# A two-layer hybrid decoder step on one core: the four group passes of layer 0 written as a loop whose passes overlap

## The chip, the cores and the metric

The kernel runs on one core of one Trainium2 chip. The metric is the device time of that core in microseconds (us), from the start of the program to its end, so lower is better. The engines are named as the profile names them: PE is TensorE (matmuls, and PEld its weight loads), DVE is VectorE, ACT is ScalarE, POOL is GpSimd, and SP is SyncE, which here only issues DMAs. Each engine works through its own list of instructions strictly in order. Semaphores are the only link between the engines: `wait_ge(s, n)` holds an engine, with everything behind it, until `s` has reached `n`.

## The reference

520 tokens (512 of a prompt and 8 decoding samples) with 1024 features pass through layer 0, a Mamba-2 mixer, and layer 1, a gated short convolution, and a last RMSNorm. Only layer 0 is touched by the change:

```python
def ssd_mixer(h, conv_buf, ssm_state, w_in, conv_w, conv_b, dt_bias, A_log, Dskip, norm_w, w_out):
    proj = h @ w_in
    z, xBC, dt = proj[..., :D_INNER], proj[..., D_INNER:D_INNER + SSD_CONV_DIM], proj[..., D_INNER + SSD_CONV_DIM:]
    xBC, new_buf = causal_dwconv(xBC, conv_buf, conv_w)      # 4 taps, per channel
    xBC = jax.nn.silu(xBC + conv_b)                          # -> xs, Bm, Cm
    dt = jax.nn.softplus((dt + dt_bias).astype(jnp.float32))
    A = -jnp.exp(A_log.astype(jnp.float32))
    y, new_state = ssd_chunked(xs, dt, A, Bm, Cm, ssm_state) # per chunk of 128 tokens
    y = y + Dskip[:, None] * xs
    y = y.reshape(b, L, D_INNER) * jax.nn.silu(z)
    y = grouped_rmsnorm(y, norm_w, SSD_GROUPS)               # one norm for each of 4 groups
    return y @ w_out, new_buf, new_state
```

All data is float32. `ssd_chunked` has, for each of 32 heads, a product within chunks of 128 tokens, the states of the chunks, a recurrence over the four chunks, and a product of the earlier state with C.

## The kernel before

**Numbers in halves.** Features lie on the partitions and tokens along the free axis, 520 columns as two halves of 260. Each float32 operand of a large matmul is split into a rounded "high" part (`whi`, `hhi`, `yhi`) and the rest (`wlo`, `hlo`, `ylo`), and a product is three matmuls: high by high, high by low, low by high. The high part of a weight chunk is a copy on ACT (L475, `split_next` and `split_out`), the low part a subtraction on DVE (L826, `next_low`).

**Chunks.** The weights come as chunks of 512 KB, numbered in the order of the table `LAYER0`. A chunk is 48 matmuls of 260 columns (L1348 for the projections B, C, x0 to x3, z0 to z3 of a group; L1380 for `o0` to `o3`, the output projection of the group before). SP loads chunk n into `raw[n % 2]` when chunk n-2 has been split into both parts, and the split parts lie in four slots, so chunk n+4 is split when PE has finished chunk n. The results go to two pairs of PSUM banks in turn (`PAIR`), and a pair must be evacuated before PE may write it again: projections by ACT (L556 to L560, `evac_conv`, or `evac_z`), outputs by DVE, which adds them to the residual (L942 and L943, `residual0`; an `o` chunk takes two turns, one for each half of its 256 columns).

**Passes.** Layer 0 is a loop over the four groups, written out in the program. In a pass, each of B, C, x0 to x3 goes through evacuation, the first tap and a tanh on ACT, and three taps (L958, `conv`) and a `silu` (L967) on DVE. Then for each q from 0 to 3 (two heads): `turn(q)` on PE transposes x, `weigh_dt` on DVE and `weigh` on POOL make `xd` and `xdd`; `within(q)` on PE has the chunk states (L1438) and the product within chunks (L1447, with `em`, which ACT makes and DVE masks in `causal`, L981); `recur` on DVE (L985 and L989) runs the recurrence; `across(q)` on PE (L1457) adds the earlier state, which DVE weighs and adds in `add_earlier`; `gate` on DVE (L1040) multiplies with silu(z) (L1033). The samples' state is scaled on ACT (L622), gets its new term by POOL (L402, `inject`) and DVE (L1022, `sample_add`), and is read by POOL (L407, `read_out`) and DVE (L1026, `sample_out`). The squares of the gated y are summed on POOL (`add_squares`, L424), PE adds them over the partitions (L1391, `group_sums`), ACT makes the root (L460 to L466, `logs` and `roots`), DVE scales (L923, `norm_scale`) and splits y (L930, `y_low`); the `o` chunks of the next pass need it.

**The order.** Nothing but the order of the calls sets what stands where on an engine. In the kernel before, all four gates of a group come before the first conv of the next group on DVE, and the squares' sums come on PE after chunks B and C of the next group. The steps that turn dt into decays (`dt_v` and `dt_s` count them) stand on DVE, ACT and PE (`columns`) before anything of the first pass that follows chunk C.

## Time and profile before

| | us |
|---|---|
| median of 3 runs | 1053.88 (1052.34 to 1056.37) |
| the profiled execution | 1050.48 |
| its span, first to last instruction | 1048.8 |
| PE busy | 920.6 (88%) |
| DVE busy | 667.7 (64%) |
| ACT busy | 477.4 (46%) |
| POOL busy | 164.0 (16%) |
| mean granted clock of PE | 0.942 of full |

Busy times are sums of the recorded instructions of an engine. Matmuls overlap in the records, so a single one lasts longer there than it holds the engine; what a chunk costs is read from the start of its first matmul to the start of what follows. The granted clock is given as a share of full speed: 1.0 is 2.4 GHz, and the other level, 1.2 GHz, is 0.5, so 0.90 in a stretch says that PE ran a fifth of it at the lower level.

### The profile page before, as it was taken

The page shows a single profiled execution, that of the slowest core. Times are in us where ns is not written, and L with a number is a line of the kernel's source. Part 1 is how long each engine was busy: PE and PEld are TensorE (multiplying, and loading weights), DVE is VectorE, ACT ScalarE, POOL GpSimd, SP SyncE. Part 2 cuts the span into 40 slices and gives each one's busy share as a digit, 9 for nine tenths or more (in the row PEclk, how much of TensorE's full clock was granted, in tenths as well). Part 3 has the DMA queues.
Part 4 walks back from the last instruction along what each step waited for, and adds up shares of the span by engine and source line. Part 5 has one row for each costly group of instructions (what it writes and reads, how often), then busy time and mean ns, then how long its engine had stood idle before and what let it go on. Part 6 is the DMA issues. An engine that isn't in the chain of part 4 may idle for free.

```text
span 1048.8 us, 19245 instructions
## 1 busy us (share of the span) xinstructions
PE 920.6 (88%) x7371; PEld 900.7 (86%) x7371; DVE 667.7 (64%) x1072; ACT 477.4 (46%) x885; POOL 164.0 (16%) x101
## 2 busy tenths in 40 slices
PE   5899688688787888868689999999999999989996
PEld 5698687688786878868679999999999999989996
DVE  5679987856868579687945454554445455463543
ACT  5477656534465354665434443232333233243444
POOL 6303540213402234022700000000000000000000
PEclk7899889899898898989879999999999999999999
DMA  7135444343443434434312243223323322331212
GB/s 187 44 113 171 127 135 114 119 123 84 123 121 124 123 83 124 119 125 144 106 43 79 62 122 98 80 84 108 88 83 97 100 80 80 103 97 62 101 58 82
DMA packets 162923, 107.98 MB, mean 103 GB/s; under 512 B 5024, under 2 KB 155068, under 8 KB 162300
## 3 DMA queue, kind: packets, MB, share of 16 engines
q1 hardware_dynamic: 123876, 76.15, 24.9%
q10 hardware_dynamic: 38592, 30.54, 10.0%
q0 software_dynamic: 400, 0.55, 0.3%
q8 instruction: 35, 0.57, 0.2%
q14 instruction: 20, 0.16, 0.0%
HBM read 95.35 MB, written 12.14 MB: 102 GB/s over the span
## 4 chain that ended last, share of the span: by engine, by line
PE 57%; DVE 24%; ACT 6%; issue 6%; POOL 2%; DVEq 0%; POOLq 0%; ACTq 0%
PE bank L1348 43%; PE bank L1528 9%; DVE acc L958 5%; DVE wlo L826 4%; PE bank L1380 4%; DVE zh L1033 2%; DVE turned L989 2%; DVE sample L1022 1%; DVE yr L1026 1%; DVE xd L972 1%; ACT whi L475 1%; ACT thx L570 1%; ACT em L594 1%; POOL sample L402 1%; DVE dtx L1016 1%
## 5 line engine op out<-in xcount | busy, mean ns | idle before, releaser
L1348 PE MATMUL bank<-hhi,whi 128*128 128x260 f32 x1664 | 347.4, 291 | 39.0 <-DVE xT L943 34.3
L1348 PE MATMUL bank<-hlo,whi 128*128 128x260 f32 x1664 | 342.0, 288 | 0.0
L1348 PE MATMUL bank<-hhi,wlo 128*128 128x260 f32 x1664 | 341.4, 287 | 0.0
L1348 PEld LDWEIGHTS bank<-hhi,whi 128*128 128x128 f32 x1664 | 265.0, 195 | 44.7 <-DVE xT L943 36.1
L1348 PEld LDWEIGHTS bank<-hlo,whi 128*128 128x128 f32 x1664 | 264.0, 194 | 0.0
L1348 PEld LDWEIGHTS bank<-hhi,wlo 128*128 128x128 f32 x1664 | 263.4, 193 | 0.0
L475 ACT ACTIVATE whi<-raw 128x1024 fp32r<-128x1024 f32 x136 | 143.6, 1056 | 231.3 <-PE bank L1348 151.3
L826 DVE TENSOR_TENSOR wlo<-raw,whi 128x1024 fp32r<-128x1024 f32 x132 | 171.5, 1301 | 43.6 <-ACT whi L475 41.6
L1380 PE MATMUL bank<-yhi,whi 128*128 128x260 f32 x256 | 55.6, 300 | 15.6 <-issue 5.0
L958 DVE SCALAR_TENSOR_TENSOR acc<-ext,colA,acc 128x544 f32<-128x544 f32 x72 | 66.4, 922 | 3.4 <-ACT acc L564 1.7
L1380 PEld LDWEIGHTS bank<-yhi,whi 128*128 128x128 f32 x256 | 42.0, 201 | 17.2 <-issue 9.3
L407 POOL TENSOR_TENSOR sample<-sample 128x1024 f32<-128x1024 f32 x16 | 43.5, 2717 | 83.4 <-DVE sample L1022 83.4
L394 POOL TENSOR_TENSOR xdd<-xd,dte 128x512 f32<-128x512 f32 x16 | 23.4, 1460 | 210.4 <-DVE xd L972 183.4
L1528 PE MATMUL bank<-hhi,whi 128*128 128x260 f32 x256 | 52.3, 286 | 3.6 <-DVE hlo L1184 3.6
L1380 PE MATMUL bank<-ylo,whi 128*128 128x260 f32 x256 | 53.8, 293 | 0.0
L1380 PE MATMUL bank<-yhi,wlo 128*128 128x260 f32 x256 | 53.8, 293 | 0.0
L1528 PE MATMUL bank<-hlo,whi 128*128 128x260 f32 x256 | 52.1, 285 | 0.0
L1528 PE MATMUL bank<-hhi,wlo 128*128 128x260 f32 x256 | 51.9, 285 | 0.0
L475 ACT ACT_TABLE_LOAD x16 | 20.5, 1283 | 66.1 <-PE bank L1348 66.0
L594 ACT ACTIVATE em<-abc,acol 128x128 f32<-128x128 f32 x128 | 39.0, 388 | 13.8 <-PE bank L1447 10.2
L1528 PEld LDWEIGHTS bank<-hhi,whi 128*128 128x128 f32 x256 | 39.9, 191 | 3.8 <-issue 3.8
L402 POOL TENSOR_TENSOR sample<-sample,dtx 128x1024 f32<-128x1024 f32 x16 | 36.6, 2289 | 35.7 <-DVE yr L1026 29.6
(227 smaller groups left out, 1218.3 us busy)
## 6 DMA issues: line engine op xcount, KB each, us to landing
raw<-in_sc_w_in SPq DMA_DIRECT2D x64, 512.0 KB, 4.0
raw<-in_ssd_w_in SPq DMA_DIRECT2D x40, 512.0 KB, 3.9
abc<-a_rows ACTq DMA_DIRECT2D x16, 512.0 KB, 4.2
sample<-in_state_ssm ACTq DMA_DIRECT2D x16, 512.0 KB, 5.5
out_new_ssm_s<-sample ACTq DMA_DIRECT2D x16, 512.0 KB, 3.5
raw<-in_ssd_w_out SPq DMA_DIRECT2D x16, 512.0 KB, 3.4
raw<-in_sc_w_out SPq DMA_DIRECT2D x16, 512.0 KB, 3.5
sample<-bc_rows ACTq DMA_DIRECT2D x4, 1024.0 KB, 4.7
```

The costliest lines, as they stand in the source:

```text
L394: pool.tensor_tensor(xdd[:, :, :].rearrange("p c (h d) -> p c h d", h=2), xd[:, :, :].rearrange("p c (h d) -> p c h d", h=2), scale, ALU.m ...
L402: pool.tensor_tensor(tdec[:, :, :], bcbc[:, :, 0, :], dtx[:, q % 2, :].unsqueeze(2).broadcast_to([P, NB, NS]), ALU.mult).then_inc(t1_done, 1)
L407: pool.tensor_tensor(tdec[:, :, :], st[:, q % 2, :].rearrange("p (b n) -> p b n", n=NS), bcbc[:, :, 1, :], ALU.mult).then_inc(t2_done, 1)
L475: act.activation(whi[:, slot, :], raw[:, slot % RAW, :], ACT.Copy).then_inc(hi_done, 1)
L594: e = act.activation(em[:, h, c * Q:(c + 1) * Q], abc[:, h, c * Q:(c + 1) * Q], ACT.Relu, scale=-1.0, bias=acol[:, c, ds(g * 8 + (2 * q + ...
L826: dve.tensor_tensor(wlo[:, slot, :], raw[:, slot % RAW, :], whi[:, slot, :].bitcast(F32), ALU.subtract).then_inc(lo_done, 1)
L958: t = dve.scalar_tensor_tensor(acc[:, :], row[:, k:k + CONV0], cw0(k, tile), acc[:, :], ALU.mult, ALU.add)
L989: dve.scalar_tensor_tensor(hs[:, c, h * HD:(h + 1) * HD], hs[:, c - 1, h * HD:(h + 1) * HD], cdbc[:, c, ds(g * 8 + (2 * q + h), 1)], bank[ ...
L1033: dve.scalar_tensor_tensor(zh[:, q % 2, :], th[:, :], 1.0, zh[:, q % 2, :], ALU.add, ALU.mult).then_inc(sz_done, 1)
L1348: mm = pe.matmul(b[:, 0:TH], w[:, slot, k * P:(k + 1) * P], h[:, k, cols], start=(k == 0 and i == 0), stop=(k == KT - 1 and i == 2))
L1380: mm = pe.matmul(bank[2 * p + hb][:, 0:TH], w[:, slot, k * 256 + part * P:k * 256 + (part + 1) * P], y[:, k, hb * TH:(hb + 1) * TH], start ...
L1528: mm = pe.matmul(bank[2 * i + hb][:, 0:TH], w[:, c % SLOT, kk * 512 + i * P:kk * 512 + (i + 1) * P], h[:, r, hb * TH:(hb + 1) * TH], start ...
```

## The change

Layer 0's passes are written as one loop on each engine, whose body begins in the middle of pass g and ends in the middle of pass g+1. Every step takes the pass as an argument and does nothing outside of 0 to 3. The steps themselves are the same instructions, with three differences: a chunk's two halves are now separate calls (`out_part`), the split of a chunk on ACT (`split`) and the first tap (`first_tap`) are calls of their own that can stand away from the evacuation, and `within` is divided into `chunk_states` and `within`. Only `MIDDLE` and `LAST` of the chunk order change: the `o` chunks stand between x3 and z3, one after each z (two of the last pass are named l2 and l3). Waits are added where the order no longer implies them. The dt steps become nine small calls; those that PE, ACT and DVE did before x0 now stand between the first chunks' convolutions. Layer 1, the start and the end are as they were.

```diff
-MIDDLE = ["B", "C", "x0", "x1", "x2", "o0", "x3", "o1", "z0", "o2", "z1", "o3", "z2", "z3"]
-LAST = ["B", "C", "x0", "x1", "x2", "o0", "x3", "o1", "z0", "z1", "z2", "z3", "o2", "o3"]
+MIDDLE = ["B", "C", "x0", "x1", "x2", "x3", "o0", "z0", "o1", "z1", "o2", "z2", "o3", "z3"]
+LAST = ["B", "C", "x0", "x1", "x2", "x3", "o0", "z0", "o1", "z1", "z2", "z3", "l2", "l3"]
...
+            for g in range(-1, GROUPS):
+                proj(g, "z2")
+                chunk_states(g, 2)
+                out_part(g, "o3", 0)
+                turn(g, 3)
+                within(g, 2)
+                out_part(g, "o3", 1)
+                proj(g, "z3")
+                across(g, 2)
+                chunk_states(g, 3)
+                proj(g + 1, "B")
+                out_part(g, "l2", 0)
+                across(g, 3)
+                within(g, 3)
+                proj(g + 1, "C")
+                proj(g + 1, "x0")
+                if g == -1:
+                    spread_decays()
+                out_part(g, "l2", 1)
+                if g == -1:
+                    columns()
+                if g == 3:
+                    turn_tails()
+                group_sums(g)
+                proj(g + 1, "x1")
+                turn_B(g + 1)
+                out_part(g, "l3", 0)
+                turn_bc(g + 1)
+                proj(g + 1, "x2")
+                turn(g + 1, 0)
+                cb_products(g + 1)
+                proj(g + 1, "x3")
+                out_part(g, "l3", 1)
+                chunk_states(g + 1, 0)
+                out_part(g + 1, "o0", 0)
+                turn(g + 1, 1)
+                within(g + 1, 0)
+                out_part(g + 1, "o0", 1)
+                across(g + 1, 0)
+                proj(g + 1, "z0")
...
+            def evac_conv(g, e):
...
+                act.wait_ge(proj_done, NUMBER[g, CONVED[e]] + 1)
+                if g * 6 + e > 1:
+                    act.wait_ge(conv_done, g * 6 + e - 1)
...
+            def split(g, what):
+                if (g, what) not in NUMBER:
+                    return
+                n = NUMBER[g, what]
+                act.wait_ge(proj_done, n + 1)
                 high(n + SLOT, n % SLOT, ((n + SLOT) // RAW + 1) * 16)
...
+                gate(g - 1, 3)
+                conv(g, 0)
+                silu(g, 0)
+                if g == -1:
+                    dt_bias()
+                next_low(g - 1, "z3")
+                next_low(g, "B")
+                conv(g, 1)
+                norm_scale(g - 1, 0)
+                if g == 0:
+                    decays_to_end()
+                silu(g, 1)
+                if g == 0:
+                    by_channel()
```

Three places of the new order follow. The first is DVE where pass 1 ends and pass 2 begins. In the rows, `sample` and `yr` are the samples' state and its sum, `ybuf<-ybuf,zh` the gate, `acc` the taps, `turned` the silu of B or C, `ybuf<-ybuf,colB,sqs` the norm's scaling. Before:

```order
L1026 TENSOR_REDUCE yr<-sample 128x1024
L1029 TENSOR_TENSOR ybuf<-ybuf,yr 128x8
L1040 TENSOR_TENSOR ybuf<-ybuf,zh 128x520
L958 SCALAR_TENSOR_TENSOR acc<-ext,colA,acc 128x544 x3
L967 SCALAR_TENSOR_TENSOR turned<-thx,acc 128x544
L826 TENSOR_TENSOR wlo<-raw,whi 128x1024
L958 SCALAR_TENSOR_TENSOR acc<-ext,colA,acc 128x544 x3
L967 SCALAR_TENSOR_TENSOR turned<-thx,acc 128x544
```

And after the change, at the same place:

```order
L1302 TENSOR_REDUCE yr<-sample 128x1024
L1306 TENSOR_TENSOR ybuf<-ybuf,yr 128x8
L1322 TENSOR_TENSOR ybuf<-ybuf,zh 128x520
L1131 SCALAR_TENSOR_TENSOR acc<-ext,colA,acc 128x544 x3
L1152 SCALAR_TENSOR_TENSOR turned<-thx,acc 128x544
L1014 TENSOR_TENSOR wlo<-raw,whi 128x1024 x2
L1131 SCALAR_TENSOR_TENSOR acc<-ext,colA,acc 128x544 x3
L1160 SCALAR_TENSOR_TENSOR ybuf<-ybuf,colB,sqs 128x520
L1152 SCALAR_TENSOR_TENSOR turned<-thx,acc 128x544
L1160 SCALAR_TENSOR_TENSOR ybuf<-ybuf,colB,sqs 128x520 x2
```

The conv of B still stands right behind the last gate. What moved is the scaling, now mixed with the silu of C, and two low parts that stand behind B's silu.

The second place is ACT at the same seam: `ext` and `tail` are the evacuation, `acc` the first tap, `whi` a high part, `thx` the tanh. Before:

```order
L560 ACTIVATE ext<-cst 128x8x3
L564 ACTIVATE acc<-ext,colA 128x544
L475 ACTIVATE whi<-raw 128x1024
L570 ACTIVATE thx<-acc 128x544
L556 ACTIVATE ext<-bank 128x260
```

And after the change:

```order
L595 ACTIVATE ext<-cst 128x8x3
L604 ACTIVATE acc<-ext,colA 128x544
L591 ACTIVATE ext<-bank 128x260
L592 ACTIVATE ext<-bank 128x252
L593 ACTIVATE ext<-bank 128x8
L594 ACTIVATE tail<-bank 128x11
L595 ACTIVATE ext<-cst 128x8x3
L506 ACTIVATE whi<-raw 128x1024 x2
L747 DMA out_new_ssm_s<-sample 128x8x128
L657 DMA abc<-a_rows 128x1024
L611 ACTIVATE thx<-acc 128x544
```

B's tanh now stands behind C's evacuation and two high parts.

The third place is DVE at the first `o` chunk of pass 2: `xT` is the residual that frees a pair of banks, `turned<-turned,cdbc,bank` the recurrence, `em` the mask, `xs` the silu of an x chunk. Before:

```order
L958 SCALAR_TENSOR_TENSOR acc<-ext,colA,acc 128x544 x3
L942 TENSOR_TENSOR xT<-xT,bank 128x260
L943 TENSOR_TENSOR xT<-xT,bank 128x260
L981 TENSOR_TENSOR em<-em,turned 128x1024
L967 SCALAR_TENSOR_TENSOR xs<-thx,acc 128x544
L942 TENSOR_TENSOR xT<-xT,bank 128x260
L943 TENSOR_TENSOR xT<-xT,bank 128x260
```

And after the change:

```order
L1131 SCALAR_TENSOR_TENSOR acc<-ext,colA,acc 128x544 x3
L1235 COPY turned<-bank 128x128
L1239 SCALAR_TENSOR_TENSOR turned<-turned,cdbc,bank 128x64 x6
L1184 TENSOR_TENSOR xT<-xT,bank 128x260
L1185 TENSOR_TENSOR xT<-xT,bank 128x260
L1014 TENSOR_TENSOR wlo<-raw,whi 128x1024
L1295 TENSOR_TENSOR sample<-sample 128x1024
L1215 TENSOR_TENSOR xd<-bank,dtcol 128x512
```

The two residuals that stood together, an `em` mask and a silu apart, are now spread, and the first stands behind the recurrence of q = 0; on PE, `turn(1)`, `within(0)`, the other half of the chunk and `across(0)` stand between the first half and z0, the next user of its banks.

## Rows read from the trace of the kernel before

**Rows 1.** Busy time by stretch: length, PE, PEld, DVE, ACT, POOL, clock, DMA, GB/s.

```profile
36.00:146.00 110.00, 91.75 (x744) 87.38 (x742) 95.46 (x143) 67.32 (x163) 38.32 (x19) 0.92 0.45 133
146.00:278.00 132.00, 106.36 (x830) 103.20 (x830) 97.25 (x144) 67.45 (x158) 33.51 (x18) 0.91 0.40 114
278.00:410.00 132.00, 107.00 (x830) 103.58 (x830) 98.13 (x146) 67.44 (x158) 34.80 (x18) 0.90 0.41 114
410.00:526.00 116.00, 88.32 (x690) 85.15 (x691) 92.55 (x137) 65.66 (x153) 35.63 (x18) 0.90 0.39 117
575.00:936.00 361.00, 360.06 (x2994) 359.60 (x2993) 184.62 (x351) 120.94 (x116) 0.00 (x0) 1.00 0.31 90
```

**Rows 2.** Groups by line, PE, 146 to 526 us: busy, mean ns | idle before.

```profile
L1348 PE MATMUL bank<-hhi,whi 128*128 128x260 f32 x448 | 100.7, 309 | 34.3 <-DVE xT L943 34.3
L1380 PE MATMUL bank<-yhi,whi 128*128 128x260 f32 x176 | 37.7, 297 | 11.9 <-issue 5.0 <-ACT ext L560 4.3 <-ACT zh L579 2.6
L1438 PE MATMUL bank<-xdd,turned 128*128 128x128 f32 x96 | 13.6, 287 | 6.1 <-POOL xdd L394 6.1
L1391 PE MATMUL bank<-sqs,ones 128*128 128x260 f32 x13 | 7.1, 690 | 21.4 <-POOL sqs L424 21.4
```

**Rows 3.** The chain that ended last: start, us, what.

```profile
320.64 8.78 PE bank L1348 x48
...
369.58 5.98 PE bank L1380 x48
375.56 5.74 PE bank L1348 x48
```

**Rows 4.** Timeline of PE, one step of q in pass 2.

```profile
329.26 0.27 PE L1286 MATMUL bank<-ident,turned 128*128 128x128 f32 x1
...
332.46 0.49 PE L1380 MATMUL bank<-yhi,whi 128*128 128x260 f32 x2
```

**Rows 5.** Groups by line and shape, DVE, 272 to 404 us.

```profile
L826 DVE TENSOR_TENSOR wlo<-raw,whi 128x1024 fp32r<-128x1024 f32 x15 | 22.6, 1510 | 0.3 <-ACT whi L475 0.3
...
L1033 DVE SCALAR_TENSOR_TENSOR zh<-th,zh 128x520 f32<-128x520 f32 x5 | 9.6, 1912 | 0.0
...
L1022 DVE TENSOR_TENSOR sample<-sample 128x1024 f32<-128x1024 f32 x4 | 4.9, 1219 | 1.8 <-POOL sample L402 1.8
...
L923 DVE SCALAR_TENSOR_TENSOR ybuf<-ybuf,colB,sqs 128x520 f32<-128x520 f32 x4 | 2.8, 754 | 2.3 <-ACT sqs L466 2.3
```

**Rows 6.** Timelines of POOL and DVE in pass 2: three meetings, one without.

```profile
337.65 2.36 POOL L407 TENSOR_TENSOR sample<-sample 128x1024 f32<-128x1024 f32 x1 [15.99 <-DVE sample L1022]
...
338.09 1.95 DVE L1016 TENSOR_TENSOR dtx<-xs,dtch 128x8 f32<-128x8 f32 x1
...
354.56 3.30 POOL L407 TENSOR_TENSOR sample<-sample 128x1024 f32<-128x1024 f32 x1 [5.03 <-DVE sample L1022]
...
355.53 2.88 DVE L1033 SCALAR_TENSOR_TENSOR zh<-th,zh 128x520 f32<-128x520 f32 x1
...
372.24 0.69 DVE L1033 SCALAR_TENSOR_TENSOR zh<-th,zh 128x520 f32<-128x520 f32 x1
...
389.72 2.42 POOL L407 TENSOR_TENSOR sample<-sample 128x1024 f32<-128x1024 f32 x1 [1.34 <-DVE sample L1022]
389.88 1.49 DVE L989 SCALAR_TENSOR_TENSOR turned<-turned,cdbc,bank 128x64 f32<-128x64 f32 x6
```

**Rows 7.** High parts on ACT, and the weights' DMA, from the page.

```profile
L475 ACT ACTIVATE whi<-raw 128x1024 fp32r<-128x1024 f32 x136 | 143.6, 1056 | 231.3 <-PE bank L1348 151.3
...
raw<-in_ssd_w_in SPq DMA_DIRECT2D x40, 512.0 KB, 3.9
```

**Rows 8.** Timeline of DVE at the start of pass 0.

```profile
48.71 0.81 DVE L899 TENSOR_TENSOR em<-ident,sm 32x640 f32<-32x640 f32 x1
...
54.58 2.43 DVE L958 SCALAR_TENSOR_TENSOR acc<-ext,colA,acc 128x544 f32<-128x544 f32 x3 [1.70 <-ACT acc L564]
```

**Rows 9.** The chain again, from the last group's sums into layer 1.

```profile
525.70 2.10 PE bank L1391 x4
...
539.03 7.29 PE bank L1380 x48
...
570.24 12.49 PE bank L1348 x102
```

More of the change, by code:

```diff
@@ new lines, in _ @@
+            next_low(3, "o0")
+            sample_add(3, 1)
+            sample_x(3, 2)
+            silu_z(3, 0)
+            residual0(3, "o1", 1)
+            skip(3, 1)
+            weigh_dt(3, 2)
+            gate(3, 0)
+            next_low(3, "z0")
+            silu(3, 5)
+            next_low(3, "o1")
+            weigh_earlier(3, 1)
+            sample_out(3, 1)
+            add_earlier(3, 1)
+            causal(3, 2)
+            next_low(3, "z1")
+            recur(3, 2)
+            sample_add(3, 2)
@@ new lines, in out_part @@
+                pe.wait_ge(pair_free[p], turn + 1)
+                for k in range(STEPS):
+                    pe.wait_ge(yg_hi, (g - 1) * STEPS + k + 1)
+                    pe.wait_ge(yg_lo, (g - 1) * STEPS + k + 1)
+                    for i, (w, y) in enumerate(((whi, yhi), (whi, ylo), (wlo, yhi))):
+                        for hb in range(2):
+                            mm = pe.matmul(bank[2 * p + hb][:, 0:TH],
+                                           w[:, slot, k * 256 + part * P:k * 256 + (part + 1) * P],
+                                           y[:, k, hb * TH:(hb + 1) * TH],
+                                           start=(k == 0 and i == 0), stop=(k == STEPS - 1 and i == 2))
@@ new lines, in cb_products @@
+            def cb_products(g):
+                if g not in PASSES:
+                    return
+                pe.wait_ge(silu_done, g * 6 + 3)
+                if g == 0:
+                    pe.wait_ge(dt_v, 23)
+                else:
+                    pe.wait_ge(rec, g * 28)
+                for c in range(NC):
+                    mm = pe.matmul(bank[5][:, c * Q:(c + 1) * Q], BT[:, c * Q:(c + 1) * Q], CT[:, c * Q:(c + 1) * Q],
+                                   start=True, stop=True)
+                mm.then_inc(cb_done, 1)
@@ new lines, in chunk_states @@
+            def chunk_states(g, q):
+                if g not in PASSES:
+                    return
+                i = g * STEPS + q
+                pe.wait_ge(xdd_done, i + 1)
+                pe.wait_ge(bs_done, g + 1)
+                if q == 0:
+                    pe.wait_ge(cbm_done, g + 1)
+                else:
+                    pe.wait_ge(rec, 7 * i)
+                for c in range(NC):
+                    mm = pe.matmul(bank[5][:, c * P:(c + 1) * P], Bs[:, c, :], xdd[:, c, :], start=True, stop=True)
+                mm.then_inc(s_done, 1)
@@ new lines, in within @@
+            def within(g, q):
+                if g not in PASSES:
+                    return
+                i = g * STEPS + q
+                pe.wait_ge(m_done, i + 1)
+                pe.wait_ge(xd_done, i + 1)
+                if q == 0:
+                    pe.wait_ge(bcd_done, g + 1)
+                else:
+                    pe.wait_ge(yd_done, 2 * i)
+                for c in range(NC):
+                    for h in range(2):
+                        mm = pe.matmul(bank[6][h * HD:(h + 1) * HD, c * Q:(c + 1) * Q], xd[:, c, h * HD:(h + 1) * HD],
+                                       em[:, h, c * Q:(c + 1) * Q], start=True, stop=True)
+                mm.then_inc(sd_done, 1)
@@ new lines, in across @@
+            def across(g, q):
+                if g not in PASSES:
+                    return
+                i = g * STEPS + q
+                pe.wait_ge(rec, 7 * (i + 1))
+                pe.wait_ge(yo_done, i + 1)
+                pe.wait_ge(fin_done, i + 1)
+                if i == 0:
+                    pe.wait_ge(dt_s, 8)
+                elif q == 0:
+                    pe.wait_ge(ln_done, g + 1)
+                transpose(bank[7][:, 0:NS], hs[:, NC - 1, :])
+                for c in range(1, NC):
+                    mm = pe.matmul(bank[7][:, c * Q:(c + 1) * Q], hs[:, c - 1, :], CT[:, c * Q:(c + 1) * Q],
+                                   start=True, stop=True)
+                mm.then_inc(o_done, 1)
```

1475 lines of the change are left out of this document (860 added, 615 removed).

## The prediction

> **What bounds the kernel now.** I read the table of stretches first, cut at the places where PE sums the squares of a group, since each pass comes through that place once [rows 1]. It shows three kinds of stretch. Layer 1 (575 to 936 us) has PE busy for 360.1 of 361 us at clock 1.00: nothing there can be gained by an order, and the change does not touch it. The four passes of layer 0 are different. In pass 1 (146 to 278) and pass 2 (278 to 410), 132 us each, PE is busy for 106.4 and 107.0 us at a granted clock of 0.91 and 0.90, and DVE for 97.3 and 98.1. So neither engine is full, and they stop each other. Only the first pass has DVE near its limit: 95.5 us of 110.
>
> Next the groups of PE over 146 to 526 us, for what it waits for [rows 2]: 34.3 us for DVE's residual, which frees a pair of banks, 21.4 us for POOL's sums of squares, 11.9 us before `o` chunks, 6.1 us for `xdd`. That is 73.7 us over three passes. Then the chain, for what a wait costs afterwards [rows 3]: a chunk takes 5.74 us, but the chunk that begins at 320.64, behind a long wait for the residual, takes 8.78. The chunk at 369.58 takes 5.98, so a short wait leaves the clock where it was. A wait is thus paid for twice when it is long: itself, and up to 3.0 us of a chunk at the lower level, 1.2 GHz.
>
> **What the floor of a pass is.** A middle pass has 14 chunks of 5.74 us, 80.4 us. One step of q (across, chunk states, within, transpose) goes from 329.26 to 332.46, 3.2 us [rows 4], four times 12.8. The sums take 2.1 [rows 9], and B's transposes and the products of B and C about 1 (estimate: half as many small matmuls as a step, less the rest). That is 96.3 us. A second way gives the same: 107.0 us busy at clock 0.90 is 96.3 at full clock [rows 1]. DVE's work is 98 us as it stands, of which some is time in which POOL held it up: the 15 low parts take 1.51 us in the mean, where an operation of the same size and kind (L1022) takes 1.22, and the silus of z take 1.91 where one that met nobody takes 0.69 [rows 5, 6]. These two groups alone are 4.4 + 6.1 = 10.5 us; with other groups of that kind I take 15 us (estimate), so DVE's own work is about 83 us a pass, and POOL's is 35.
>
> **The change, part by part.** No matmul, no DVE operation on data and no DMA is added or removed, apart from the division of calls; a wait that is satisfied costs less than I can read. So all of the gain is in when things stand.
>
> *The residuals.* Before, the two residuals of o0 stand behind a conv and a mask, and PE has only within(0) and turn(1) before it needs the banks. After, half a chunk (2.9 us) and a step's matmuls lie between each half and the next user of its pair, and DVE does a residual between other work. I laid PE's new order out at 5.74 a chunk, 2.87 a half and 3.2 a step, with time 0 at x2, and then DVE's list beside it, each step at its duration in the timeline of pass 2 (a low part 1.14, a conv 2.42, a residual 0.67, a recurrence 1.7, start to start, where they met nobody). The first half of o0 is done at 16.6; DVE gets to its residual by 20.9, behind recur(0); z0 wants the banks at 21.7. The second half is done at 20.9, the residual at 26.1, wanted by o1 at 28.4. o1's: 33.5 against 35.6, and 39.6 against 41.3. So the 34.3 us go, but with slack of 0.8 to 2.3 us, and POOL's collisions will eat this in some places. *The squares.* The gate of q = 3 comes at 81.2 in this frame, POOL ends about 3 us later, and PE sums at 88.3, since chunk x0 has moved ahead of the sums. The 21.4 us go in passes 1 and 2. *xdd and the chunk states*: 12.2 against 12.8, and 26.5 against 27.5: gone, with almost no slack.
>
> *What becomes late next.* At the seam ACT makes B's tanh behind C's evacuation and two high parts of 1.06 us each [rows 7], so DVE, whose silu of B stands right behind B's conv, waits until about 3.7 us after PE ends C; behind it in DVE's list stand the low parts for x1 and x2, and PE waits for them if they slip by 2 us. I read 2.6 us of waiting for DVE there. The norm's scaling stood behind the root before, with 2.3 us of waiting [rows 5], and the same 2.4 us stay. The recurrence of q = 3 waits for its chunk states behind z3, about 3 us in this frame, which later collisions fill. So a pass is 98.1 us of DVE as now (the collisions are those of now: the same operations meet) + 2.4 + 2.6 + 3 for all places where PE and DVE miss each other by little, 106 us. PE has then some 10 us of idle time in pieces too short to lower the clock. Ends of this: PE's floor, 96.3, and DVE's 83 with all of POOL's 35 on top, 118. I take 106 since the walk found no wait of PE over 2.5 us, and since 98.1 is measured and not argued.
>
> *How POOL and DVE collide* decides between these. POOL's `read_out` ran from 337.65 to 340.01, and DVE's product of 8 columns at 338.09 took 1.95 us and ended when POOL did; the silu of z at 355.53 took 2.88 and ended within 0.6 us of POOL. But the recurrence at 389.88, one of whose inputs is in PSUM, ran its usual 1.49 us beside POOL [rows 6]. The Trainium skill, page "SBUF — State Buffer", section "SBUF: two separate sides", states that the two engines take one pair of ports as an exclusive lock, where DVE has two inputs in SBUF. By that rule the trace agrees, and it speaks against this change: the fuller DVE is, the more of POOL's time falls on it.
>
> *The last pass* (410 to 526) has DVE busy for 92.6 of 116 us. The same additions give 92.6 + 8 = 100.6, less 2.4 for a conv that moves across the cut, plus 2 for the end, where nothing of a next pass fills the gaps: 100. *The first pass* is DVE's: it starts its first conv at 54.58 now, since ACT evacuates B only behind the dt steps, while its last dt product starts at 48.71 and ends at 49.5 [rows 8]. After, ACT evacuates B and C early, and conv B can start at about 50. The decays it then does between convs take as long as before. I take 4.6 us; the ends are 0, if the added waits for `dt_s` and `dt_v` hold PE's transposes, and 10, if the pass also loses its few gaps. *The end* of layer 0, 525.7 to 570.24 [rows 9], has a chunk of 7.29 us at the lower clock and a last low part that PE awaits; spreading it gives 3 us, with ends of 0 and 8.
>
> **The sum.** 4.6 + (132 - 106) x 2 + (116 - 100) + 3 = 75.6 us. The profiled execution took 1050.5 us, so 974.9; the median of the runs shown is 3.4 us above it, so **978 us**. With the waits at 106 +/- 4 a pass and the last pass alike, its own range is 965 to 992.
>
> **Rivals.** *A, DVE is the bound and POOL falls on it whole* (chance 0.17). A pass is 83 + 35 = 118, the last 92.6 - 15 + 35.6 = 113: 4.6 + 28 + 3 + 3 = 39 us, 1015. For it: the low parts and the silus of z show how often the two meet already [rows 5]; against: the recurrence went past POOL unharmed [rows 6], and so should the residuals and other readers of PSUM. The lock that the Trainium skill states on the page "SBUF — State Buffer" is this rival's mechanism, and taken alone it gives these 1015 us, where the measured busy time gives 978.
>
> *B, PE's floor is reached* (0.13). 97 us a pass and 92 for the last: 4.6 + 70 + 24 + 8 = 107, 947. For it: the walk shows PE never waiting if DVE has its durations without collisions; against: the slacks of 0.3 to 2.3 us are less than one collision of 2.2.
>
> *C, slower, by the raw slots* (0.04). Two chunks share the slots in turn, so for each slot a round is a landing of 3.9 us, the high part's 1.06 and the low part's 1.22 [rows 5, 7], 6.2, plus the time a loaded chunk waits for its turn in ACT's list and then in DVE's. A round serves two chunks of PE time. While these queue waits stay below 2 x 6.9 - 6.2 = 7.6 us, they are free. If ACT, which now waits for a `proj_done` at each split, and DVE add 12.8 us between them, a round takes 19, a pass 133, and the kernel ends at 1050 to 1065. In my walk the worst round (split of o3 to its low part, 18 us) has one such wait and not seven.
>
> *D, no change* (0.03): the waits go to other places in the same amount, a pass of 131 us, within 0.5%, about what a measurement of this kernel can tell from no change.
>
> **How the numbers follow.** Own case 0.63, A 0.17, B 0.13, C 0.04, D 0.03. The range reaches to A's and B's times: **948 to 1015**. Faster by more than 0.5%: 0.63 + 0.17 + 0.13 = 0.93; slower 0.04; same 0.03.
>
> **What would show it.** In the changed profile, the sums of the squares should lie some 106 us apart (before: 132), with the granted clock in these stretches at 0.97 or more, and DVE at 92% or more of each pass. PE's wait for the residual should fall from 34.3 to under 12 us, and for POOL's sums from 21.4 to a few, nearly all in the last pass. DVE's longest regular waits should be the silu of B for its tanh and the scaling for the root. First conv at 50. I would be wrong if the low parts and silus of z, in the mean, take much longer than 1.51 and 1.91 us (A), if PE waits for `wlo` or ACT for `raw` in each pass (C), or if a long wait at the seam keeps the clock at 0.9.

## The result, and the profile after

The changed kernel takes **948.41 us** (median of 4 runs, 945.86 to 951.9), the kernel before 1053.11 us in the same series (4 runs, 1052.09 to 1056.37): a ratio of 0.9003, 95% interval 0.8968 to 0.9039, 104.7 us less. The forecast was 978 with a range of 948 to 1015, so the time lies at the very bottom of the range: direction right, size too small. The profiled execution took 951.9 us, the longest of the four; its span is 950.2, the mean granted clock 0.972 (before 0.942).

The table of stretches, cut in each pass at the sums of the squares (columns as in [rows 1]), and layer 1 in the last row:

```profile
36.00:137.00 101.00, 94.98 (x795) 92.58 (x792) 93.60 (x142) 67.77 (x168) 36.90 (x19) 0.97 0.51 144
137.00:237.30 100.30, 97.23 (x832) 94.93 (x831) 97.14 (x145) 67.06 (x158) 32.69 (x17) 1.00 0.52 148
237.30:337.00 99.70, 97.17 (x832) 94.85 (x831) 96.84 (x144) 67.02 (x158) 32.56 (x17) 1.00 0.52 153
337.00:431.40 94.40, 76.77 (x644) 73.92 (x642) 90.74 (x137) 63.20 (x147) 33.76 (x17) 0.94 0.46 140
...
480.00:840.00 360.00, 356.01 (x2959) 355.28 (x2957) 187.96 (x356) 124.10 (x122) 0.00 (x0) 1.00 0.31 92
```

A middle pass holds the same 832 or so matmuls and 97 us of DVE's busy time as before, in 100 us instead of 132. PE's busy time itself falls by 9 to 10 us, since the clock there is 1.00 and no longer 0.90. In layer 1 PE is still 99% busy at clock 1.00.

What PE waits for, its groups over 36 to 470 us, against [rows 2], and then its waits in pass 2 one by one:

```profile
L1700 PE MATMUL bank<-hhi,whi 128*128 128x260 f32 x654 | 136.0, 289 | 5.4 <-DVE wlo L1014 5.4
L1744 PE MATMUL bank<-yhi,whi 128*128 128x260 f32 x256 | 54.7, 295 | 2.2 <-DVE ylo L1169 1.6 <-issue 0.6
L1835 PE MATMUL bank<-em,xd 128*64 128x128 f32 x256 | 18.9, 293 | 10.3 <-DVE em L1224 10.3
...
L1757 PE MATMUL bank<-sqs,ones 128*128 128x260 f32 x16 | 5.2, 459 | 8.7 <-POOL sqs L444 8.7
```

```profile
240.01 0.47 PE L1700 MATMUL bank<-hhi,whi 128*128 128x260 f32 x2 [1.66 <-DVE wlo L1014]
...
268.24 0.33 PE L1638 MATMUL bank<-ident,turned 128*128 128x128 f32 x1 [0.50 <-DVE turned L1239]
...
278.99 1.09 PE L1835 MATMUL bank<-em,xd 128*64 128x128 f32 x16 [0.21 <-DVE em L1224]
```

The wait for the residual, 34.3 us, is gone altogether; the wait for POOL's sums, 21.4, is 8.7 and lies in the last pass alone. In pass 2 PE loses 2.4 us to waits, none of which lowers the clock.

Last, DVE's groups over the two middle passes (137 to 337 us), against [rows 5]:

```profile
L1014 DVE TENSOR_TENSOR wlo<-raw,whi 128x1024 fp32r<-128x1024 f32 x28 | 36.5, 1309 | 0.0
...
L1224 DVE TENSOR_TENSOR em<-em,turned 128x1024 f32<-128x1024 f32 x8 | 16.5, 2067 | 0.0
L1312 DVE SCALAR_TENSOR_TENSOR zh<-th,zh 128x520 f32<-128x520 f32 x8 | 13.3, 1664 | 0.0
...
L1257 DVE TENSOR_SCALAR ybuf<-xs,dch 128x8 f32<-128x8 f32 x8 | 6.2, 769 | 0.0
...
L1160 DVE SCALAR_TENSOR_TENSOR ybuf<-ybuf,colB,sqs 128x520 f32<-128x520 f32 x8 | 5.9, 755 | 1.1 <-ACT sqs L497 1.1
...
L1152 DVE SCALAR_TENSOR_TENSOR turned<-thx,acc 128x544 f32<-128x544 f32 x4 | 2.9, 723 | 1.4 <-ACT thx L611 1.4
L1235 DVE COPY turned<-bank 128x128 f32<-128x128 f32 x8 | 2.3, 282 | 1.0 <-PE bank L1820 1.0
```

DVE's waits on other engines in two passes are the three shown, 3.5 us together.

DVE begins its first conv 4.9 us earlier than in [rows 8], at the row

```profile
49.70 2.41 DVE L1131 SCALAR_TENSOR_TENSOR acc<-ext,colA,acc 128x544 f32<-128x544 f32 x3
```

and the chain from the last sums into layer 1 (start, us, what) answers to [rows 9]; its first chunk still runs at the lower clock, 7.37 us:

```profile
431.38 2.10 PE bank L1757 x4
433.47 7.37 PE bank L1744 x48
...
484.73 5.30 PE bank L1700 x42
```

The gain by stretch, from the marks, which are the starts of the sums (before 146.9, 279.5, 411.0, 525.7; after 137.0, 237.3, 337.0, 431.4), and the start of layer 1's steady chunks (584.5 and 484.7): first pass 9.9 us, middle passes 32.3 and 31.7, last pass 20.4, end of layer 0 5.5. Their sum is 99.8 us. The spans differ by 98.6, since what follows takes 1.2 us longer in the changed kernel.

### The profile page after: what moved, and what is told of

The parts are those of the page before. It is cut to its first block, busy times and chain, and to the rows that moved or that the text cites. A ratio compares the mean times of both kernels' runs of the same rounds, so it can differ in the third digit from the quotient of the medians.

```text
span 950.2 us, 19548 instructions
## 1 busy us (share of the span) xinstructions
PE 893.1 (94%) x7371; PEld 877.8 (92%) x7371; DVE 663.9 (70%) x1072; ACT 475.5 (50%) x885; POOL 157.4 (17%) x101
## 4 chain that ended last, share of the span: by engine, by line
PE 52%; DVE 1%; ACT 1%; issue 0%; POOLq 0%; POOL 0%; DVEq 0%; ACTq 0%
PE bank L1700 39%; PE bank L1935 10%; PE bank L1744 3%; DVE zh L1312 0%; ACT xT L934 0%; POOLq L86 0%; PE bank L1757 0%; DVE ybuf L1628 0%; ACT sqb L774 0%; DVE hlo L1536 0%; ACT L491 0%; DVE yr L1302 0%; ACT whi L506 0%; POOL sqb L432 0%; PE bank L1964 0%
## 5 line engine op out<-in xcount | busy, mean ns | idle before, releaser
L1700 PE MATMUL bank<-hhi,whi 128*128 128x260 f32 x1664 | 339.2, 285 | 6.4 <-DVE wlo L1014 5.4
L1700 PE MATMUL bank<-hhi,wlo 128*128 128x260 f32 x1664 | 336.3, 284 | 0.0
L1700 PE MATMUL bank<-hlo,whi 128*128 128x260 f32 x1664 | 335.6, 283 | 0.0
L1700 PEld LDWEIGHTS bank<-hhi,whi 128*128 128x128 f32 x1664 | 257.8, 190 | 9.1 <-issue 7.6
L1700 PEld LDWEIGHTS bank<-hhi,wlo 128*128 128x128 f32 x1664 | 257.5, 189 | 0.0
L1700 PEld LDWEIGHTS bank<-hlo,whi 128*128 128x128 f32 x1664 | 257.3, 189 | 0.0
L1014 DVE TENSOR_TENSOR wlo<-raw,whi 128x1024 fp32r<-128x1024 f32 x132 | 166.1, 1260 | 38.3 <-ACT whi L506 36.0
L1131 DVE SCALAR_TENSOR_TENSOR acc<-ext,colA,acc 128x544 f32<-128x544 f32 x72 | 62.6, 870 | 1.8
L1935 PE MATMUL bank<-hhi,whi 128*128 128x260 f32 x256 | 53.0, 289 | 3.6 <-DVE hlo L1536 3.6
L1935 PE MATMUL bank<-hlo,whi 128*128 128x260 f32 x256 | 52.5, 287 | 0.0
L1935 PE MATMUL bank<-hhi,wlo 128*128 128x260 f32 x256 | 52.4, 287 | 0.0
L1935 PEld LDWEIGHTS bank<-hhi,whi 128*128 128x128 f32 x256 | 40.5, 194 | 3.8 <-issue 3.8
L416 POOL TENSOR_TENSOR sample<-sample,dtx 128x1024 f32<-128x1024 f32 x16 | 38.8, 2424 | 27.2 <-issue 17.8
L1935 PEld LDWEIGHTS bank<-hlo,whi 128*128 128x128 f32 x256 | 40.7, 194 | 0.0
L1935 PEld LDWEIGHTS bank<-hhi,wlo 128*128 128x128 f32 x256 | 40.4, 193 | 0.0
```

The lines of the kernel that those rows point to most:

```text
L416: pool.tensor_tensor(tdec, bcbc[:, :, 0, :], dtx[:, q % 2, :].unsqueeze(2).broadcast_to([P, NB, NS]), ALU.mult).then_inc(t1_done, 1)
L1014: dve.tensor_tensor(wlo[:, slot, :], raw[:, slot % RAW, :], whi[:, slot, :].bitcast(F32), ALU.subtract).then_inc(lo_done, 1)
L1131: t = dve.scalar_tensor_tensor(acc[:, :], row[:, k:k + CONV0], cw0(k, tile), acc[:, :], ALU.mult, ALU.add)
L1700: mm = pe.matmul(b[:, 0:TH], w[:, slot, k * P:(k + 1) * P], h[:, k, cols], start=(k == 0 and i == 0), stop=(k == KT - 1 and i == 2))
L1935: mm = pe.matmul(bank[2 * i + hb][:, 0:TH], w[:, c % SLOT, kk * 512 + i * P:kk * 512 + (i + 1) * P], h[:, r, hb * TH:(hb + 1) * TH], start ...
```

## Experiments

The open questions: what holds a pass at 100 us now, PE's list of work, or DVE's with POOL's interference; which moves brought the gain; and why the waits that the forecast put on DVE did not come. Each expectation spells out its own theories. Times are medians; ratios are to the kernel before in the same series (1051.81 us for the first four, 1050.34 for the next four, 1051.02 for the last four). The changed kernel itself came out at ratios of 0.9003 and 0.9035 in two series, 3 us apart, so a difference of medians across series is uncertain by about as much; the marks of its two profiled executions agree within 0.2 us.

**1. The dt steps in one block again** (dt_first). All of the changed kernel, but the dt chain stands ahead of the loop on each engine, and the sample columns and decays between chunk C and x0:

```diff
+            dt_exp()
+            dt_log()
+            early_high()
+            ...
             for g in range(-1, GROUPS):
```

> The changed kernel, but all dt steps stand in one block before the loop on ACT and DVE, and PE does columns and decays between C and x0 of pass 0, as in the kernel before. Theory 1 (the head's gain is that the first conv starts at 49.7 instead of 54.6 us, and what follows is dense on DVE either way): first sums of squares at 142, against 137.0 in the changed kernel and 146.9 before; the later intervals stay 100, 100, 94 us; the whole 5 us above the changed kernel, 953. Theory 2 (all 9.9 us of the head come from the dt steps): first sums at 147, the whole 958. Theory 3 (the dt steps were hidden anyway): first sums at 137 to 138, the whole 949.

Measured 953.8 us (953.31 to 954.87), ratio 0.9064 [0.9044, 0.9085]. DVE's first conv starts at 53.53 instead of 49.70, PE waits for ACT's evacuation once more, and the first mark is 141.8, 4.8 us later than 137.0:

```profile
52.67 0.80 PE L1685 MATMUL bank<-hhi,whi 128*128 128x260 f32 x2 [1.85 <-ACT ext L595]
```

So the spreading is worth 5 us up to the first mark. At the last mark (433.5 against 431.4) 2.1 us of it are left: the later passes take 100.5, 98.3 and 92.9 us, the last two 1.4 and 1.5 us less than in the changed kernel, with DVE busy for 1.3 and 0.8 us less. The medians differ by 5.4. The other 5.1 of the 9.9 us that the first pass gained lie elsewhere in it; at its end alone PE waited 3.70 us for POOL's sums before, and does not now.

**2. The sums of the squares where they were** (sums_early), ahead of chunk x0 in the first three passes:

```diff
+                if g < 3:
+                    group_sums(g)
                 proj(g + 1, "x0")
...
-                group_sums(g)
+                if g == 3:
+                    group_sums(g)
                 proj(g + 1, "x1")
```

> The changed kernel, but PE sums the squares of passes 0 to 2 before chunk x0 and not behind it, where the kernel before had it (behind B and C). Theory 1 (the sums waited because PE reached them before DVE's last gate; a chunk of 5.7 us in between covers this): PE waits 3 to 5 us for POOL at each of the three places, and each interval becomes 3 to 5 us longer, 103 to 105, since PE has only 3 us to spare in a pass: the whole 957 to 963. Theory 2 (DVE sets the pace and PE has slack to catch up): the wait of PE shows, but the intervals stay at 100 to 101, the whole 948 to 951.

Measured 957.18 us (955.01 to 958.43), 0.909 [0.9066, 0.9115], the lower end of what was expected. PE waits at each of the three places (4.21, 3.61 and 5.00 us), and the group shows the old wait:

```profile
L1757 PE MATMUL bank<-sqs,ones 128*128 128x260 f32 x16 | 6.5, 547 | 20.4 <-POOL sqs L444 20.4
```

11.7 us more of waiting here cost 7.8 us at the last mark and 8.8 in the medians, since other waits shrink (for `wlo` from 5.4 to 0, for `em` from 10.3 to 8.2): DVE caught up while PE stood. The first three marks stand a chunk earlier in this order, 101.7 and 101.6 us apart, nearer to theory 2's 100 to 101 than to theory 1's 103 to 105.

**3. One residual half about 5 us later** (res_pair): the first half of o0 is added when the second is.

```diff
                 recur(g, 0)
-                residual0(g, "o0", 0)
...
+                residual0(g, "o0", 0)
                 residual0(g, "o0", 1)
```

> The changed kernel, but DVE does the residual of the first half of o0 together with that of the second half, about 5 us later, behind an operation on the samples, xd, the earlier state and the skip, so that z0's banks come free late. Theory 1 (the place of the residual is a large part of the gain): PE waits about 4 to 5 us before z0 in passes 1 to 3 and the intervals become 104, 104, 97: the whole 10 to 14 us above the changed kernel, 958 to 962. Theory 2 (DVE's list alone sets the pace, and PE's wait is made up before DVE needs PE again): waits of 4 us show on PE, but the intervals grow by less than 1.5 us each, the whole 949 to 952.

Measured 962.76 us (960.55 to 964.42), 0.9152 [0.9128, 0.9176]. PE waits 4.4 us in each of three passes. The two middle passes take 105.2 and 104.5 us; the last takes 94.6, against 94.4 in the changed kernel:

```profile
276.35 0.80 PE L1700 MATMUL bank<-hhi,whi 128*128 128x260 f32 x2 [4.39 <-DVE xT L1185]
```

The two matmuls behind it take 0.80 us together, where two behind a short wait take 0.47 (at 240.01 above): the lower clock again (granted 0.50 from 276.3 to 280). The last mark comes 9.2 us later than in the changed kernel for 13.2 us of waiting, since PE's waits for `em` fall from 10.3 to 5.5; the medians differ by 14.3. One of eight residual halves a pass is enough for it. The slack of this half is small, as the walk had it (0.8 us): in pass 2 of the changed kernel the residual ends at 268.86 and z0 begins at 269.00.

**4. The kernel before, with four residuals earlier on DVE** (before_res): in each pass o0's and o1's stand one or two calls further ahead; nothing else is touched.

```diff
+                        residual0(g, 0, 0)
                     conv(4, g * 4 + 2)
-                        residual0(g, 0, 0)
```

> The kernel before, with one thing of the change alone: four calls of the residual on DVE (o0 and o1, both halves, passes 1 to 3) stand earlier: the first half of o0 ahead of the conv of x2 and the second ahead of the mask, those of o1 around the silu of x3. Theory 1 (places of the residuals are a third of the gain): PE's wait for the residual falls from 34.3 to about 15 us, with the lower clock behind these waits gone too, and each of the three intervals becomes 6 to 8 us shorter: the whole 1029 to 1035. Theory 2 (without the overlap of the passes the wait only moves to the next place, xdd or the silus): 1045 to 1053.

Measured 1037.72 us (1034.22 to 1038.43), 0.9848 [0.982, 0.9875], 14 us less, between the two theories. A pass takes 127 to 128 us. In pass 2 the two waits of 5.44 and 5.01 us are now:

```profile
312.75 0.51 PE L1349 MATMUL bank<-hhi,whi 128*128 128x260 f32 x2 [2.43 <-DVE xT L943]
...
333.26 0.80 PE L1349 MATMUL bank<-hhi,whi 128*128 128x260 f32 x2 [5.45 <-DVE xT L943]
```

One halves, the other stays; over the three passes the wait falls from 34.3 us to 24.5 and not to 15. Moving calls inside the old, closed pass gives a seventh of the gain.

**5. Less work for PE** (pe_cut): the changed kernel without the third product (`wlo` by `hhi`) in the four z chunks of a pass. The z values are less exact; everything else is computed.

```diff
-for i, (w, h) in enumerate(((whi, hhi), (whi, hlo), (wlo, hhi))):
+for i, (w, h) in enumerate(((whi, hhi), (whi, hlo), (wlo, hhi))[:2 if cut else 3]):
```

> The changed kernel with less work on PE: the four z projections of each pass leave out the product of the low weight part with the high input part (16 of 48 matmuls each, 1.9 us a chunk, 7.6 us a pass), all other engines as they are; z is less exact. Theory 1 (DVE's list, 97 us busy with its meetings with POOL, sets the pace of a pass, with PE's 96 only just below): the intervals fall from 100 to 98, that is 1 to 3 us each, the whole 941 to 946. Theory 2 (PE's floor sets the pace): each interval falls by 6 to 7.6 us, 93, the whole 921 to 926.

**6. Less work for POOL** (pool_cut): the changed kernel with POOL's two products over the samples (`inject`, `read_out`) made on one sample of eight. It leaves out the state update and output of seven samples; DVE's and ACT's instructions are as before.

```diff
-pool.tensor_tensor(tdec, bcbc[:, :, 0, :], dtx[...].broadcast_to([P, NB, NS]),
+pool.tensor_tensor(tdec[:, 0:1, :], bcbc[:, 0:1, 0, :], dtx[...].broadcast_to([P, 1, NS]),
```

> The changed kernel with less work on POOL: its two operations on the samples' state (inject and read_out) work on one of the eight samples only, so that POOL's busy time in a pass falls from 33 to about 15 us and DVE is held up less; the new state and y of the other samples are left out, and a fill of the buffer is added at the start. Theory 1 (DVE sets the pace and 14 us of its 97 are time held up by POOL): DVE's busy time in a middle pass falls to 86 to 89 us, the interval to PE's floor, 97, the first sums come 8 us earlier, the last interval is 85: the whole 925 to 932. Theory 2 (PE sets the pace everywhere): under 3 us of change, 945 to 949.

**7. Both cuts** (both_cut), leaving out what 5 and 6 leave out.

> Both cuts together (POOL's two operations on one sample of eight, and PE without the third product of z). Theory 1 (each engine is a floor of its own, 2 to 3 us apart): middle intervals of 89 to 91 us, much less than either cut alone gives, the whole 905 to 915. Theory 2 (PE alone): the same as with PE's cut alone, near 921 to 926. Theory 3 (DVE alone): the same as with POOL's cut alone.

**8. POOL's cut in the kernel before** (before_pool_cut), the same seven samples left out.

> The kernel before, with the same cut on POOL (inject and read_out on one sample of eight). Theory 1 (before, neither engine was full, a pass was held by the chain from engine to engine at the seam and at the residuals, and only part of the time DVE lost to POOL lay on that chain): intervals from 132 to 122 to 127, the whole 1015 to 1035. Theory 2 (before was DVE's as well): each interval falls by all of the 10 to 14 us of meetings and more, with 1000 or less for the whole.

In the order above, measured: pe_cut **949.82** (948.75 to 951.21), ratio 0.904 [0.9016, 0.9064]; pool_cut **922.77** (921.09 to 923.45), 0.8773 [0.8749, 0.8797]; both_cut **911.81** (910.51 to 913.29), 0.8673 [0.8648, 0.8698]; before_pool_cut **1026.29** (1023.14 to 1028.45), 0.977 [0.9742, 0.9797]. The two middle passes in the first three, cut at their sums (same columns as above). First pe_cut, then pool_cut, then both_cut:

```profile
137.00:237.00 100.00, 91.52 (x767) 88.86 (x767) 97.26 (x145) 67.27 (x158) 33.26 (x18) 0.98 0.50 147
237.00:336.40 99.40, 91.60 (x766) 88.85 (x766) 96.88 (x145) 67.20 (x158) 32.52 (x17) 0.98 0.53 153
```

```profile
128.50:225.50 97.00, 96.57 (x834) 94.82 (x833) 87.07 (x147) 68.06 (x159) 20.26 (x17) 1.00 0.55 153
225.50:321.80 96.30, 96.30 (x832) 94.86 (x831) 85.57 (x145) 67.36 (x159) 19.53 (x17) 1.00 0.55 160
```

```profile
128.00:220.20 92.20, 89.12 (x768) 87.15 (x767) 87.42 (x147) 67.05 (x159) 20.54 (x17) 1.00 0.57 162
220.20:311.60 91.40, 88.98 (x768) 87.33 (x767) 85.86 (x145) 67.59 (x160) 21.56 (x17) 1.00 0.58 168
```

These six rows settle the bound. With 64 matmuls fewer a pass, PE has 8 us of gaps and the pass is as long as ever: theory 1's 941 to 946 us did not come, and DVE, busy 97 of 99.4 us, sets the pace. With POOL's products short, DVE needs 86 to 87 us, PE is busy for 96.3 of 96.3 us, and the pass is PE's. With both cuts neither is full and a pass takes 91.4 to 92.2. So the two bounds of the changed kernel lie only 3.4 us apart in a middle pass. Of pool_cut's gain 8.4 us lie before the first mark, 3.4 in each middle pass and 12.9 in the last pass; its 922.77 us are below theory 1's range, while both_cut and before_pool_cut lie within theirs. In the kernel before, POOL's cut takes 24.1 us off; in the changed one 24 to 28 (its ratios of 0.9003 and, in the last series, 0.9035, less pool_cut's 0.8773, times 1050). What the cut takes off DVE's busy time is about the same in both kernels: in the kernel before it falls from 97.3 and 98.1 us a middle pass to 88.6, in the changed one from 97.1 and 96.8 to 87.1 and 85.6. How the meetings reach the whole time is not the same. In the kernel before, PE's wait for POOL's sums also falls, from 21.4 to 7.7 us, and its wait for the residual only from 34.3 to 28.0, so POOL's own delay counted there too.

**9. Trying for more.** The changed kernel once more (after_again), the product of eight columns moved from DVE to ACT (small_act), the low part of z3 ahead of B's silu (low_first), and both with two places of the last pass reordered (lean).

> The changed kernel once more, to stand beside the three that follow on the same chip. Both theories: 946 to 950 us, the marks of its group sums near 137, 237, 337 and 431 us.

> The changed kernel with the product of eight columns of each tile (128x8, 0.86 us in the mean on DVE, 16 times) on ACT, with a semaphore of its own. Theory 1 (DVE sets the pace, and these 0.86 us are its own): 13.7 us leave DVE, of which the middle passes can give 2.8 each before they meet the 96.9 us that the kernel with less on POOL took; first and last pass 2 each; 938 to 941 us. Theory 2 (the short product only waits out a POOL instruction that the next two-input instruction of DVE would wait for instead): the time moves on to the neighbours, low parts or masking rise by as much; 945 to 948 us. The busy time of DVE in a middle pass tells them apart: 3 us less, or as before.

```diff
-                dve.tensor_scalar(yt[:, SEQ:T], dec_conv(xs[:, q % 2, :]), d, None, ALU.mult).then_inc(yd_done, 1)
+                act.activation(y_tile(g, q)[:, SEQ:T], dec_conv(xs[:, q % 2, :]), ACT.Copy, scale=dch[:, i:i + 1]).then_inc(ys8_done, 1)
```

> The changed kernel with the low part behind z3 placed ahead of the silu of B on DVE, at each seam. Theory 1 (DVE sets the pace; PE's 1.7 to 2.1 us wait for that low part at the seam is paid by DVE's lag anyhow): only the 0.7 us that the silu waits for its tanh is gained, 2 us in all at most; 946 to 948 us. Theory 2 (PE's wait at the seam is on the path): 1.7 to 2.1 us in each of three seams, 5 to 6 us; 942 to 944 us.

```diff
                 conv(g, 0)
+                next_low(g - 1, "z3")
                 silu(g, 0)
-                next_low(g - 1, "z3")
```

> Both edits together, and in the last pass the masking of tile 2 two places earlier and the last silu of z behind the sum over samples. Theory 1: middle passes 97, the last pass 3 to 4 us shorter (of its waits of 4.8 for the mask and 8.7 for the squares), 933 to 938 us. Theory 2 (time moves on to the neighbours): 940 to 944 us.

```diff
             weigh_earlier(3, 1)
+            causal(3, 2)
             sample_out(3, 1)
             add_earlier(3, 1)
-            causal(3, 2)
...
-            silu_z(3, 3)
...
             sample_out(3, 3)
+            silu_z(3, 3)
```

Measured: after_again 950.03 (947.62 to 951.68), 0.9035 [0.9018, 0.9052]; small_act **945.32** (943.87 to 947.66), 0.8998 [0.8981, 0.9015]; low_first 951.46 (948.92 to 952.26), 0.9042 [0.9026, 0.9058]; lean 945.53 (944.68 to 946.74), 0.8993 [0.898, 0.9005]; 5 runs each.

low_first did what it was to do and gained nothing, 951.46 us where both theories had less. PE's wait at the seam of pass 2 fell from 1.66 to 0.21 us, and came back behind it (the second row is new, the third was 0.50):

```profile
239.09 0.47 PE L1700 MATMUL bank<-hhi,whi 128*128 128x260 f32 x2 [0.21 <-DVE wlo L1014]
246.21 0.39 PE L1638 MATMUL bank<-ident,turned 128*8 128x128 f32 x2 [0.71 <-DVE turned L1152]
...
269.12 0.33 PE L1638 MATMUL bank<-ident,turned 128*128 128x128 f32 x1 [1.20 <-DVE turned L1239]
```

DVE's waits moved as well: the norm's scaling now waits 5.1 us for the root in three passes instead of 1.7, and the silus of B and C 1.3 instead of 3.4. Here, where DVE is late everywhere, this move in its order only chose where PE waits.

small_act is the fastest version, 4.7 us below the changed kernel beside it, in theory 2's range of 945 to 948 and not in theory 1's. In the two middle passes DVE is busy for 95.8 and 95.4 us, 1.3 and 1.5 less than before, where theory 1 had 3. The 16 products took 13.7 us on DVE. DVE's busy time up to the last sums falls by 7.1 us (378.2 to 371.1) and the last mark comes 5.5 us earlier (431.2 to 425.7). The difference is at the neighbours, DVE's groups of small_act over 36 to 430 us:

```profile
L1029 DVE TENSOR_TENSOR wlo<-raw,whi 128x1024 fp32r<-128x1024 f32 x50 | 65.7, 1318 | 0.0
...
L1337 DVE TENSOR_TENSOR ybuf<-ybuf,zh 128x520 f32<-128x520 f32 x16 | 12.9, 807 | 0.5
```

Beside it the low parts took 1284 ns and the gates 690: 1.7 and 1.9 us moved on to them, as theory 2 has it. Another 2.3 us moved to `dtx` (L1287, also 128x8, both inputs in SBUF), 7.4 to 9.7 us. In pass 0 of after_again the product of eight columns takes 1.12 us at 113.31 and `dtx` behind it 0.15; in small_act `dtx` takes the 1.12 itself, at 111.19. lean, at 945.53 us, is above both of its theories and adds nothing: the last pass is 92.3 us instead of 92.5.

## Why the prediction was right, and where it was too small

- **The number.** The forecast was 29.6 us too long. Profiled execution against profiled execution it is 23.0 (974.9 against 951.9). The rest is which execution was profiled: the 3.4 us added for the median had the other sign, since the changed kernel's profiled execution is 3.5 above its median. The own case's range, 965 to 992, missed. The stated range held because it reached down to rival B's time, and that part is luck.
- **The bound and its cause.** Right. PE and DVE stopped each other; the waits for the residual and for POOL's sums were what went, and the clock came back with them: 1.00 in the middle passes (0.97 or more was forecast). In the last pass it is 0.94, below that; PE waits 4.78 us for `em` and 8.73 for the squares there.
- **PE's floor, 96.3 us a pass.** Right: pool_cut's second pass is 96.30 us long with PE busy for 96.30, its first 97.0. One term was read at the lower clock: the four matmuls of the sums take 2.1 us in [rows 9] and 1.04 in the changed kernel's middle passes.
- **DVE's 98.1 us "as now".** Right: 97.1 and 96.8. Over the two middle passes of each kernel, the low parts (1.31 us in the mean against 1.37), silus of z (1.66 against 1.94) and gates (0.69 against 0.91) meet POOL less than before, the masking (2.07 against 1.48) and the product of eight columns (0.77 against 0.23) more. The forecast's 1.51 and 1.91 come from the window of [rows 5], which has 15 low parts and 5 silus of z where a pass has 14 and 4. That the meetings as a whole hold DVE for as long as before is shown by experiments 6 and 8.
- **"+ 2.4 + 2.6 + 3", the step that failed.** These 8 us of waiting on DVE measured 2.9 in pass 2 (99.7 less 96.8), of which 1.7 are waits for other engines: 0.6 for the root (forecast 2.4), 0.7 for the tanh of B (2.6), 0.4 for chunk states (3). The places were right, the sizes too large, each by a factor of 3.6 to 8. So a middle pass is 100 us and not 106: 12.1 us of the 24.2 us by which the stretches exceeded the forecast. The three terms failed differently.
  - *The tanh of B.* In the walk DVE was done with B's conv and waited while ACT worked off C's evacuation and two high parts. In pass 2 it is the other way round: ACT is through with them at 234.53 and waits 2.77 us for DVE, whose conv took 4.02 us instead of 2.42, beside POOL's squares (233.55 to 234.95 and 235.16 to 236.70). What DVE then waits is the tanh alone. The same conv took 3.99 us in the kernel before (at 276.08), so the meeting was already in the 98.1, while the walk took the conv at 2.42.

```profile
233.26 4.02 DVE L1131 SCALAR_TENSOR_TENSOR acc<-ext,colA,acc 128x544 f32<-128x544 f32 x3
238.00 0.73 DVE L1152 SCALAR_TENSOR_TENSOR turned<-thx,acc 128x544 f32<-128x544 f32 x1 [0.72 <-ACT thx L611]
```

```profile
233.46 1.07 ACT L506 ACTIVATE whi<-raw 128x1024 fp32r<-128x1024 f32 x1
...
237.31 0.66 ACT L611 ACTIVATE thx<-acc 128x544 f32<-128x544 f32 x1 [2.77 <-DVE acc L1131]
```

  - *The root.* The 2.4 us were carried over from the kernel before. In the new order ACT's way from the first tap of C to the root (238.82 to 243.86) begins behind B's silu, so it moves with DVE, and DVE fills nearly all of it with two low parts and a conv. low_first takes one low part out of this stretch, and the wait grows from 0.6 to 1.7 us.
  - *The chunk states.* Here an engine that sets the pace is late, and finds its input there. With DVE's load down to 86 or 87 us (pool_cut) it does reach them early, and waits 4.4 us for them in each middle pass (the third term said 3) and 3.0 and 3.5 for half chunks. For the tanh and the root it waits 0.7 and at most 0.9 there too, so DVE's lateness is not what made these two small.
- **Last pass, 16 us forecast, 20.4 measured.** The same term: 100 = 92.6 + 8 - 2.4 + 2 had the 8 us in it; measured are 94.4, with DVE busy for 90.7.
- **First pass, 4.6 forecast, 9.9 measured.** The evacuation was right (first conv at 50 forecast, 49.70 measured), and experiment 1 returns 4.8 us. What was left out are the pass's other waits, 5.1 us, among them the 3.70 before the sums. The upper bound of 10, "if the pass also loses its few gaps", was the value. (In [rows 8], 48.71 is not DVE's last dt step: seven small ones follow, until 52.9. They now stand behind B's conv.)
- **End of layer 0, 3 forecast, 5.5 measured.** Within its ends of 0 and 8.
- **Rival A** (POOL falls on DVE whole, 1015 us) fell. Its mechanism is at work, though, and what POOL's cut takes off, some 26 us, is the largest item that one experiment moved. The Trainium skill, page "SBUF — State Buffer", section "SBUF: two separate sides", calls the shared pair of ports "an exclusive lock", taken for a whole instruction. By that rule the trace agrees: silus of z take 0.69 us or, met, up to 2.89 (at 420.24, beside POOL's product at 419.79).
- **Rival B** (PE's floor, 947 us) gave nearly the measured time by another road. Its middle passes, last pass and end gained 12.1 us less than it had them, and the first pass 5.3 more. Experiment 5 shows that PE is not the bound.
- **Rivals C and D** fell: PE's waits did not merely move, and no pass grew. The sign named for C, that PE waits for `wlo` in each pass, did appear, but at 1.7 to 2.1 us once a pass, and low_first, which only moves that low part on DVE, takes it to at most 0.7.
- **How the gain divides** is settled only in part. Undone alone, the dt chain costs 5.4 us, the later sums 8.8 and one residual half's place 14.3 by the medians, 28.5 us of 104.7, each uncertain by some 3 us; at the last marks of the profiles it is 2.1, 7.8 and 9.2. The rest lies in the overlap as a whole, with all residuals, `xdd` and the chunk states, and no single undoing was tried for those. A restoration's cost is also no share of the gain: in experiments 2 and 3, part of a wait put back was taken from other waits.

## What to carry to other kernels

Where two engines stop each other, find the busy time of each in one pass: their maximum, plus at most 4%, was the middle pass here in the changed kernel and its three cuts, as soon as each result stood ahead of its need. Do not add a wait to the engine that sets the pace merely because its input comes late in a walk at undisturbed durations; ask at each place what else the input itself waits for, and whether the engine is there first. And before trimming the busiest-looking engine, cut its work in a trial: 8% of PE's matmuls taken away gave nothing here, while POOL, busy for a third of a pass, held some 26 us.

## What the runs showed of the hardware

A short product with one tensor input in SBUF is held up beside POOL too. The product of eight columns, 128x8, took 0.23 us in the mean in the kernel before (L999) and 0.86 in the changed one (L1257). In the changed kernel's timeline:

```profile
95.31 2.86 POOL L423 TENSOR_TENSOR sample<-sample 128x1024 f32<-128x1024 f32 x1 [8.13 <-DVE sample L1295]
```

```profile
96.49 1.71 DVE L1257 TENSOR_SCALAR ybuf<-xs,dch 128x8 f32<-128x8 f32 x1
```

It ends at 98.20, when POOL's product does (98.17). The reduction of 1024 columns (L1302), also with one input in SBUF, took 1.20 to 1.22 us at all eight places of the first two passes, though at 83.53 it ran beside POOL's `xdd` (83.46 to 84.51). On ACT the same 128x8 product took 290 to 328 ns in all 16 places:

```profile
L758 ACT ACTIVATE ybuf<-xs,dch x16: 290/298/328, 67.8 to 399.4; 128x8 f32<-128x8 f32 x16
```

The forecast had counted only DVE's operations with two inputs in SBUF as exposed. The Trainium skill, page "SBUF — State Buffer", section "Who interferes with whom", names `tensor_scalar` among the operations that can enter, if their operands allow it, a mode which takes both ports, and `tensor_reduce` among those that never contend on this chip. By that rule the trace agrees, in both halves, though no run shows in which mode the product ran.
